# Prompt attention of a two-layer decoder step: row maxima carried to the query operand by DMA instead of by TensorE and ScalarE

## The reference, cut to what matters

```python
s = jnp.einsum('nqhd,nkhd->nhqk', q, k) * (HEAD_DIM ** -0.5)
s = s + (c_q - c_k)                 # c: cumulated log forget values
s = jnp.where(causal, s, NEG_INF)
p = jax.nn.softmax(s, axis=-1)      # needs each row's maximum first
out = jnp.einsum('nhqk,nkhd->nqhd', p, v)
```

## Time and profile before

| what | value |
|---|---|
| median of three runs | 2565.19 (2564.46 to 2565.8) |
| the profiled execution | 2564.02 |
| its span | 2561.7 |
| granted TensorE clock, mean | 0.999 |
| TensorE busy | 2525.1, 99% |
| VectorE busy | 1808.4, 71% |
| ScalarE busy | 1048.2, 41% |
| SyncE's DMA queue | 229030 packets, 248.37 MB |

### The profile page before, as it was taken

One profiled execution on the slowest core, in us unless ns is written; L12 is line 12 of the kernel. 1 busy time (PEld: TensorE's weight loads), 2 busy tenths in 40 slices (PEclk: granted clock), 3 DMA queues, 4 the chain that ended last, 5 costly groups with the idle time before them and its releaser, 6 DMA issues.

```text
span 2561.7 us, 45919 instructions
## 1 busy us (share of the span) xinstructions
PE 2525.1 (99%) x18332; PEld 2473.7 (97%) x18332; DVE 1808.4 (71%) x2438; ACT 1048.2 (41%) x1491; POOL 24.4 (1%) x48
## 2 busy tenths in 40 slices
PE   8999999999999999999999999999999999999998
PEld 8999999999999999999999899988899999999998
DVE  5434437666688998954345898876696666899986
ACT  4111124333333323465245777765553333333333
POOL 0000000000000000000000100000000000000000
PEclk9999999999999999999999999999999999999999
DMA  3111111332353312025424656644223333433111
GB/s 120 50 41 48 43 43 40 124 101 101 102 197 105 129 63 90 6 83 168 118 77 137 141 136 167 145 127 148 92 84 101 101 101 108 178 135 135 51 51 69
DMA packets 248430, 259.42 MB, mean 101 GB/s; under 512 B 18160, under 2 KB 182960, under 8 KB 248290
## 3 DMA queue, kind: packets, MB, share of 16 engines
q1 hardware_dynamic: 229030, 248.37, 31.1%
q10 hardware_dynamic: 19260, 9.09, 1.3%
HBM read 193.86 MB, written 63.42 MB: 100 GB/s over the span
## 4 chain that ended last, share of the span: by engine, by line
PE 87%; DVE 4%; DMA 3%; ACT 2%; issue 2%; SPq 2%; ACTq 0%; DVEq 0%
PE ps L591 28%; PE ps L790 24%; PE ps L845 24%; PE ps L810 2%; DMA sums_spread<-o_and_sums 1%; PE ps L1252 1%; PE ps L1102 1%; PE ps L1167 1%; PE ps L1254 1%; PE ps L1253 1%; PE ps L1169 1%; PE ps L1460 1%; PE ps L629 1%; PE ps L692 1%; DMA inv_rows<-inv_spread 0%
## 5 line engine op out<-in xcount | busy, mean ns | idle before, releaser
L845 PE MATMUL ps<-h_op,w_op 128*128 128x268 f32 x4912 | 615.1, 286 | 2.7 <-DVE w_op L885 2.5
L845 PEld LDWEIGHTS ps<-h_op,w_op 128*128 128x128 f32 x4912 | 610.4, 189 | 3.4 <-DVE w_op L885 3.4
L591 PE MATMUL ps<-x_hi,w_hi 128*128 128x358 f32 x1248 | 277.2, 330 | 4.9 <-DVE w_lo L575 4.7
L575 DVE TENSOR_TENSOR w_lo<-w_raw,w_hi 128x1024 fp32r<-128x1024 f32 x76 | 92.8, 1221 | 257.2 <-ACT w_hi L567 257.2
L591 PE MATMUL ps<-x_hi,w_lo 128*128 128x358 f32 x1248 | 273.3, 327 | 0.0
L591 PE MATMUL ps<-x_lo,w_hi 128*128 128x358 f32 x1248 | 272.9, 327 | 0.0
L856 ACT ACTIVATE w_op<-w_op_f 128x2048 fp32r<-128x2048 f32 (+1 forms) x54 | 97.7, 1809 | 388.4 <-PE ps L845 367.6
L591 PEld LDWEIGHTS ps<-x_hi,w_hi 128*128 128x128 f32 x1248 | 213.7, 190 | 7.1 <-DVE w_lo L575 5.1
L591 PEld LDWEIGHTS ps<-x_lo,w_hi 128*128 128x128 f32 x1248 | 215.9, 189 | 0.0
L591 PEld LDWEIGHTS ps<-x_hi,w_lo 128*128 128x128 f32 x1248 | 215.6, 189 | 0.0
L1040 DVE TENSOR_TENSOR t<-ps,t 128x536 f32<-128x536 f32 x180 | 128.7, 715 | 120.2 <-PE ps L790 111.4
(11 more groups left out here) (358 smaller groups left out, 5173.6 us busy)
## 6 DMA issues: line engine op xcount, KB each, us to landing
raw_a<-in_mlp_w SPq DMA_DIRECT2D x120, 256.0 KB, 3.1
h_op_f<-h_rows SPq DMA_DIRECT2D x24, 1072.0 KB, 6.2
w_op_f<-in_mlp_w SPq DMA_DIRECT2D x24, 1024.0 KB, 7.5
h_rows<-t SPq DMA_DIRECT2D x90, 268.0 KB, 2.1
w_raw<-in_conv_w_in SPq DMA_DIRECT2D x24, 512.0 KB, 3.7
w_raw<-in_w_kv SPq DMA_DIRECT2D x16, 512.0 KB, 4.7
w_raw<-in_w_o SPq DMA_DIRECT2D x16, 512.0 KB, 3.9
k_page<-in_cache_k SPq DMA_DIRECT2D x16, 512.0 KB, 5.1
```

The lines of the kernel that those rows point to most:

```text
L575: dve.tensor_tensor(WL[:, s], RAW[:, s], WH[:, s].bitcast(F32), ALU.subtract).then_inc(w_lo, 1)
L591: mm = pe.matmul(PS[:, bank(s, g), 0:GW], w[:, s, k], x[:, k, g * GW:(g + 1) * GW], start=(k == 0 and n == 0), stop=(k == KC - 1 and n == 2))
L845: mm = pe.matmul(PS[:, 2 * p + g, 0:QW], w[:, k, P * m:P * m + P], x[:, k, QW * g:QW * g + QW], start=(k == 0 and j == 0), stop=(k == tile ...
```

## The change

- The entries "A", "B" and "C" leave `USES`: a head has 13 uses of the ring in place of 16, and no matmul with the unit matrix for the maxima. `keep_shift` and its copies on ScalarE go.
- `move_shift` comes: for each query tile one DMA from the column of `NMR` (one element of 4 bytes in each of 128 partitions; 16 for tile 0) to 128 elements of the row of `QA`. That is four DMAs for "A", three for "B" and two for "C", nine for a head and 144 in all, each waiting for the joined maxima (`nm_ready`). `logits` waits for their landing (`nm_in`) in place of `nm_kept`. The minus sign goes into the constant row of `CK` (-1.0 in place of 1.0).
- SyncE's queue issues them for heads 1 to 15: "C" of head h first, ahead of `load_cross(h + 1)`; "A" of head h+1 after `spread_sums(h - 1)`; then `load_head(h + 2)`, which stood ahead of `spread_sums` before; then "B" of head h+1; then `load_inverse(h - 1)`. For head 0 ScalarE issues them.
- `USE_AT` is written anew: slots 0 and 1 keep their products, slot 2 gets three, slot 3 two, slot 4 one, slot 5 two, slot 6 one, slot 7 none. Because 13 is odd, the bank of a use alternates from head to head.

```diff
-        "A", (7, 0, 512), "B", (7, 512, 912), (8, 16, 528), (8, 528, NPR), "C"]
+        (7, 0, 512), (7, 512, 912), (8, 16, 528), (8, 528, NPR)]
...
-JOIN_AT = {3: "A", 8: "B", 14: "C"}
-USE_AT = [(0, 1), (2, 3), (4, 5), (6, 7), (8, 9), (10, 11), (12, 13), (14,)]
+JOIN_AT = {3: "A", 8: "B", 12: "C"}
+USE_AT = [(0, 1), (2, 3), (4, 5, 6), (7, 8), (9,), (10, 11), (12,), ()]
...
-            if x in SHIFTS:
-                pe.wait_ge(nm_ready, N_SH * h + "ABC".index(x) + 1)
-                first = max_rows(SHIFTS[x][0])[0]
-                for i in SHIFTS[x]:
-                    q, rows = max_rows(i)
-                    mm = pe.matmul(PS[0:1, bank, q - first:q - first + rows], NMR[:, hh, i:i + 1], IDR[:, 0:rows],
-                                   start=True, stop=True)
...
-            act.activation(QA[h % SETS][HD:HD + 1, q0:q1], PS[0:1, bank_of(h, u), 0:q1 - q0], ACT.Copy, scale=-1.0)\
-               .then_inc(nm_kept, 1)
+        def move_shift(eng, h, x):
+
+            _, hh = head(h)
+            eng.wait_ge(nm_ready, N_SH * h + "ABC".index(x) + 1)
+            to = QA[h % SETS][HD:HD + 1].bitcast(F32)
+            for i in SHIFTS[x]:
+                q, rows = max_rows(i)
+                eng.dma_start(to[:, q:q + rows].rearrange("o (p i) -> o p i", i=1), NMR[0:rows, hh, i:i + 1].bitcast(F32))\
+                   .then_inc(nm_in[x], 16)
...
             if g == 0 or CHUNK_OF[g] != CHUNK_OF[g - 1]:
-                pe.wait_ge(nm_kept, N_SH * h + CHUNK_OF[g] + 1)
+                x = "ABC"[CHUNK_OF[g]]
+                pe.wait_ge(nm_in[x], SHIFT_IN[x] + SHIFT_COUNT[x] * (h + 1))
...
                     if h:
+                        move_shift(sp, h, "C")
                         if h + 1 < HEADS:
                             load_cross(h + 1)
-                        if h + 2 < HEADS:
-                            load_head(h + 2)
                         spread_sums(h - 1)
+                    if h + 1 < HEADS:
+                        move_shift(sp, h + 1, "A")
+                    if 0 < h and h + 2 < HEADS:
+                        load_head(h + 2)
+                    if h + 1 < HEADS:
+                        move_shift(sp, h + 1, "B")
+                    if h:
                         load_inverse(h - 1)
```

More of the change, by code:

```diff
@@ L191 @@
 SHIFTS = {"A": range(0, 4), "B": range(4, 7), "C": range(7, NT)}
-REDS = [0 if x in SHIFTS else 2 if x == "M" else 1 for x in USES]
+SHIFT_COUNT = {"A": 64, "B": 48, "C": 32}
+SHIFT_IN = {"A": 0, "B": 16, "C": 16}
+REDS = [2 if x == "M" else 1 for x in USES]
 N_RED, N_SH = sum(REDS), len(SHIFTS)
-JOIN_AT = {3: "A", 8: "B", 14: "C"}
-USE_AT = [(0, 1), (2, 3), (4, 5), (6, 7), (8, 9), (10, 11), (12, 13), (14,)]
[L196 to L199, removed]
+JOIN_AT = {3: "A", 8: "B", 12: "C"}
+USE_AT = [(0, 1), (2, 3), (4, 5, 6), (7, 8), (9,), (10, 11), (12,), ()]
+USE_AT_FIRST = [(), (0, 1, 2), (3, 4, 5), (6, 7, 8)] + USE_AT[4:]
+NORM_HEAD, NORM_USE = 1, NUSE - 2
+FIRST_USES = [(), (), (), (0, 1, 2, 3), (4, 5, 6, 7), (8, 9), (10, 11, 12), ()]
 RING = 2
@@ L490, in trunk @@
         logf_stored, c_stored = sem("logf_stored"), sem("c_stored")
+        nm_in = {"A": sem("nm_in"), "B": gate_w_loaded, "C": bf_loaded}
         lt_kept = sem("lt_kept")
@@ L1068, in ring_wait @@
                 return
[L1069 to L1072, removed]
+            pe.wait_ge(red_done, reds_through(h0, u0))
         def max_logits(h, u):
@@ L1081, in max_logits @@
             ring_wait(h, u)
-            if u == NORM_USE + RING and NORM_HEAD < h <= NORM_HEAD + G:
-                pe.wait_ge(aux_read, AX_Q + 3 * (KC - 1) + h - NORM_HEAD)
-            if x in SHIFTS:
-                pe.wait_ge(nm_ready, N_SH * h + "ABC".index(x) + 1)
-                first = max_rows(SHIFTS[x][0])[0]
-                for i in SHIFTS[x]:
-                    q, rows = max_rows(i)
-                    mm = pe.matmul(PS[0:1, bank, q - first:q - first + rows], NMR[:, hh, i:i + 1], IDR[:, 0:rows],
-                                   start=True, stop=True)
-            elif x == "M":
+            if u == 0 and NORM_HEAD + 1 < h <= NORM_HEAD + 1 + G:
+                pe.wait_ge(aux_read, AX_Q + 3 * (KC - 1) + h - NORM_HEAD - 1)
+            if x == "M":
                 for j, i in enumerate(FIRST_KEYS):
@@ L1725, in attention_scalar @@
             values_hi(0)
-            keep_shift(0, "C")
+            move_shift(act, 0, "C")
             exp_logits(1)
@@ L1731, in attention_scalar @@
                 if g == 1 and NORM_HEAD < h <= NORM_HEAD + G:
-                    root(AX_Q + 3 * (KC - 1) + h - NORM_HEAD - 1, NORM_BANK, h - NORM_HEAD - 1)
-                h, g = divmod(t - 1, NG)
-                if 0 <= h < HEADS - 1 and g in SHIFT_AT:
-                    keep_shift(h + 1, SHIFT_AT[g])
-                if 0 < h < HEADS - 1 and g == 0:
-                    keep_shift(h, "C")
-                elif h == HEADS - 2 and g == NG - 1:
-                    keep_shift(h + 1, "C")
+                    root(AX_Q + 3 * (KC - 1) + h - NORM_HEAD - 1, bank_of(h, NORM_USE), h - NORM_HEAD - 1)
                 h, g = divmod(t - 2, NG)
@@ L1980, in late_norm @@
             c = slice(g * GW, (g + 1) * GW)
-            pe.matmul(PS[:, NORM_BANK, 0:GW], heads1[:, :], SQ[U_Q][1][1][:, c], start=True, stop=False)
-            pe.matmul(PS[:, NORM_BANK, 0:GW], heads1[:, :], T2R[:, c], start=False, stop=True).then_inc(aux_done, 1)
+            b = bank_of(NORM_HEAD + g + 1, NORM_USE)
+            pe.matmul(PS[:, b, 0:GW], heads1[:, :], SQ[U_Q][1][1][:, c], start=True, stop=False)
+            pe.matmul(PS[:, b, 0:GW], heads1[:, :], T2R[:, c], start=False, stop=True).then_inc(aux_done, 1)
         def uses_at(h):
@@ L1993, in uses_of @@
                 return uses + [h - NORM_HEAD]
-            if g == 0 and 0 < h < HEADS - 1:
-                return [(h, last_shift)] + uses
-            if g == NG - 1 and h == HEADS - 2:
-                return uses + [None, (h + 1, last_shift)]
             return uses
@@ L2588, in _ @@
                 if n == 5:
-                    keep_shift(0, "A")
-                    keep_shift(0, "B")
+                    move_shift(act, 0, "A")
+                    move_shift(act, 0, "B")
                 head_root(ax(AX_Q + 3 * n, 0, 0), n == KC - 2)
@@ L3243, in norm @@
                         pe.wait_ge(red_done, reds_through(0, FIRST_USES[n][-1]))
-                        pe.wait_ge(nm_kept, sum(USES[u] in SHIFTS for u in range(FIRST_USES[n][-1] + 1)))
                     f()
```

17 lines of the change are left out of this document (4 added, 13 removed).

## The result

| | before | after |
|---|---|---|
| median, six runs each on one chip | 2565.16 (2564.46 to 2569.96) | 2588.66 (2585.76 to 2591.23) |
| ratio | | 1.009, 95% interval 1.0079 to 1.0102 |
| span of the profiled execution, mean granted clock | 2561.7, 0.999 | 2586.3, 0.996 |

The kernel is slower by 23.5, inside the range and on the side that the prediction took. Whether its reasons hold is another question.

The account below looks back on a forecast made before the run. TensorE held 87% of the chain, with VectorE nearly as busy; the moves would make SyncE's path the bound. Heads 1 to 6 add 11.4 and heads 7 to 14 add 22.3: 2564.0 + 33.7 = 2597.7, stated as 2598, range 2551 to 2608.

Parts of the forecast that it names:

- The issue time i: SyncE's queue: time from one move's issue to the next, taken as 0.91, with ends 0.38 and 1.0.
- the second rival: SyncE's queue: moves issue as from row to row, 0.59 each, so no change, 2560.7; chance 0.15.
- The chain's other terms: Round through SyncE's DMAs, `divide` and the next join: 12.7 besides seven issues, 19.0 a head; heads 1 to 6 +11.4.
- SyncE's own queue: SyncE's work per head with nine moves: 20.2 in heads 7 to 14, where it binds, adding 22.3.
- TensorE's gain of 12.3: TensorE: 7.5 of unit-matrix matmuls and 4.8 of waits go, but are worth nothing while it waits longer in each head.
- The first rival: SyncE's queue: issue is cheap, near 0.38, nothing there binds and the kernel gets faster, 2551.7; chance 0.30.
- The landing: Moves of 128 pieces of 4 bytes: each lands in 2.1, and nobody waits for it.
- The third rival: Path through "B": moves land late, binding above 4.4; at 6 a head takes 20.6, total 2613; chance 0.05.
- The ring: TensorE's slot 2: with three products it waits for VectorE's reduction, 0.74 a head, 11 for 15.
- The fourth rival: With cheap moves TensorE waits in slot 2 for VectorE's reduction, 11 against 12.3 gained: 2563, no change; chance 0.05.
- The signs named: Changed kernel's profile: issue near 870 ns, heads of 19 and 20, `divide` waiting 1.5 to 3, TensorE idle 2 to 3.
- the likeliest case: SyncE's queue: moves issue in 0.8 to 1.0, giving 2586 to 2608; chance 0.43.

Follow-up runs that it names:

- the first experiment: The changed kernel without the nine moves of each head and TensorE's waits for them, exponentials' scale a thousandth, set against the kernel before: 2564.72 (0.9996).

## Why the prediction was right, and where it was not

*The side and the mechanism.* SyncE's slack was the resource that the moves used up, and the path through it to `divide` and the next join became the bound. Shown: moves that nobody needs cost 17.9; another order of the same work, with the reciprocals a slot earlier, gives back 20.8; `divide` waits in each head; the queue waits for the join in heads 1 to 6 and not in heads 10 to 13, as the prediction divided them.

*The issue time i.* This is the term that was mis-sized: 0.91 taken from the spreading of the sums, 0.63 measured. Kind ("between a row and many partitions") was a bad guide. By the prediction's own formula 0.63 gives a chain of 17.1 and thus next to no cost in heads 1 to 6, and the second rival's "no change". That the forecast of 33.7 was only 10 too high is owed to terms that were too small on the other side.

*The chain's other terms.* In heads 1 to 14 the reading back left 1.9 after the store on average, not 1.35, because the store landed later; in head 10 it was 2.23. Also "A" stood behind the spreading of the sums, 1.01 in head 10, which the chain had left out. The landing of the reading back was sized rightly: its median is 3.7, and the 4.27 of head 10 is among the longest. I had taken the store's landing from a kernel whose queue had a pause in front of it. The experiment with small loads shows what the load does: without the bulk, the reading back left 1.5 after the store, and heads 1 to 6 take 16.96. Forecast for heads 1 to 6 was +11.4, measured +5.0.

*SyncE's own queue.* Forecast 20.2 a head in heads 7 to 14, measured 19.5 in 7 to 13; +16.9 there, and 0.7 in head 14, against +22.3 forecast. With the measured 0.63 the prediction's queue comes to 17.7, so here too something is missing. Heads 7 and 9 alone are 9.3 of the 16.9: the queue gives "C" out late there, TensorE stands for it, and the clock falls. What comes back when the queue is relieved (0.9 to 1.0 a head) comes mostly or wholly from these two heads. In the rest, relief of the queue alone is worth little.

*TensorE's gain of 12.3.* "Worth nothing then" was right, for the wrong reason: I held it to be hidden by the waits. With no transport at all 4.1 of it comes in the 13 heads, and 7.1 with the products as before. What holds back the rest was not shown; VectorE is nearly as full as TensorE, and `divide` waited 12.7 and 20.3 in these two kernels. In the traced executions the gain is given back behind the heads. The first rival (2551.7) was not reached by any median, though three executions without moves took 2551.2 to 2551.8. A gain must be followed to the end of the program.

*The landing.* The third rival was the missing part: TensorE's need for moves that had not landed is about 6.0 of the 23.5 as a difference of medians. The prediction looked only at "B". It was mostly "C" (7.5 of the 11.0 of its stops), which in heads 7 and 9 leaves behind the stores or page loads and is needed at once. From what the Trainium skill, "DMA: Bandwidth & Descriptors", Specifications, says of pieces below 512 bytes, the prediction drew a landing longer than 2.1. The 2.7 agrees, but with small loads in front it was 2.0, so no run shows a cost of the piece's size apart from what is in flight.

*The ring.* The fourth rival's wait was 8.1 in 14 places, 0.58 each. Without moves it is worth 4.2 by the medians and 3.0 by the heads; in the changed kernel taking it away gains nothing, since "B" is joined a slot later.

*The signs named.* `divide` waits in each head: seen, 1.9 on average. SyncE's wait for the reciprocals gone: 10.3 left of 100.7. Heads of 19 and 20: 17.9 and 19.5. TensorE idle 2 to 3 in each head behind `probs_lo`: 1.2 (18.7 in 15 heads, its matmuls alone). A landing near 2: 2.7. Issue near 870 ns: not seen. "The forecast is wrong if moves issue in less than 0.63": they issue in just that, and it was still slower, so that condition was wrongly drawn.

*Slips in the working.* The rows of 0.42 and of 4.8 name no releaser ("issue"); the prediction put both down to ScalarE. They are gone in the changed kernel, which fits, but no row names ScalarE. The second rival's sum counts the queue's head start as a gain; it can only cancel the 1.6, so the sum is -1.8, 2562.2. By its own terms the likeliest case runs to 2610, not 2608, and the chances add to 0.33 faster, 0.17 the same and 0.50 slower. None of this changes the forecast.

*Open.* The order of the queue and the earlier reciprocals were changed together; the second alone does not help the old kernel, but its part in the new one was not separated. Of the 0.7 by which heads 7 to 13 stay longer there, the stop for "C" in head 9 and the clock in head 10 are seen; why TensorE stood 1.17 in head 10 is not, since the row names no releaser.

## What to carry to other kernels

An idle stretch in front of a wait in a DMA queue is not free room: work put ahead of it delays everything behind it, and what is behind may close a loop through another engine. Price the loop with landings as they are under load, and then move what the loop does not need (here the large loads) out from between its parts before the change is judged. Look also for single DMAs that are needed at once and stand behind occasional work in the queue: a mean over all heads hides them. Handing small urgent DMAs to another issuer frees the issuer, not the DMA engines.

## What the runs showed of the hardware

*A stop of TensorE can cost more than its length.* In head 9 of the changed kernel TensorE stood 3.21 for "C"; the first row is its timeline, the others are windows behind it:

```profile
1590.81 0.59 PE L1160 MATMUL ps<-q_hi_ext,k_hi_ext 128*128 128x272 f32 x1 [3.21 <-DMA q_hi_ext<-row_max]
```

```profile
1591.00:1593.00 2.00, 2.00 (x8) 2.00 (x9) 0.00 (x0) 0.88 (x2) 0.00 (x0) 0.50 1.03 237
1593.00:1595.00 2.00, 2.00 (x11) 1.84 (x10) 1.10 (x3) 0.25 (x1) 0.00 (x0) 0.73 0.25 16
1595.00:1597.00 2.00, 2.00 (x17) 1.90 (x15) 1.83 (x5) 1.69 (x4) 0.00 (x0) 1.00 0.87 200
```

The granted clock is 0.50 (1.2 GHz of 2.4) behind the stop, and 1.00 again in the window from 1595: 0.50 x 2.0 + 0.27 x 2.0 = 1.5 lost on top of the 3.2. Head 7, with a stop of 2.2 for "C", has the same. That is why these two heads are the longest, 21.34 and 22.33, with a mean clock of 0.92 each:

```profile
1544.41:1565.75 21.34, 17.42 (x115) 16.42 (x113) 14.94 (x37) 11.62 (x23) 0.00 (x0) 0.92 0.63 165
1565.75:1582.65 16.90, 16.13 (x115) 15.04 (x113) 14.56 (x37) 11.50 (x23) 0.00 (x0) 1.00 0.52 115
1582.65:1604.98 22.33, 17.59 (x115) 16.50 (x113) 14.98 (x38) 11.60 (x23) 0.00 (x0) 0.92 0.57 133
```

0.08 x 43.7 = 3.5 is lost by the clock in this execution. The kernel before had 1.00 in every head of its traced execution. This is not the same in every execution: the mean clock was 0.992 to 0.996 in the six of the changed kernel and 0.995 to 0.999 in those of the kernel before that ran beside the experiments, so how much of the 23.5 is clock on average is not settled by one pair. Nor does every stop bring it: the stop of 2.7 that both kernels of the first experiment have was followed by a lower clock in one and not in the other. The prediction priced each wait by its length alone.

*Small DMAs land with the large ones around them.* The same move of half a kilobyte landed in 1.6 to 7.6. The median was 2.7 from SyncE and 2.5 with all moves on ScalarE, so the issuer makes no difference here; with the large loads cut small it was 2.0, and among the four large loads of the cross operands it was 7.2.
